# Softmax stage of a hybrid decoder layer: columns of maxima and inverse sums turned by one transpose each and spread by DMA

## The reference, cut to what is computed here

```python
z = jnp.einsum('bhqd,bhkd->bhqk', qi, k).astype(jnp.float32) * scale
causal = key_pos[None, :] <= q_pos[:, None]
p = jax.nn.softmax(jnp.where(causal, z, neg), axis=-1)
return jnp.einsum('bhqk,bhkd->bhqd', p.astype(v.dtype), v)
```

## Time and profile before

| | us |
|---|---|
| median of three runs | 2100.22 |
| the profiled execution's own time | 2099.88 |
| its span in the trace | 2098.2 |
| softmax stage, first score matmul of a turn | 1397.0 |
| softmax stage, last store issued | 1896.4 |

### The profile page before, as it was taken

One profiled execution on the slowest core, in us unless ns is written; L12 is line 12 of the kernel. 1 busy time (PEld: TensorE's weight loads), 2 busy tenths in 40 slices (PEclk: granted clock), 3 DMA queues, 4 the chain that ended last, 5 costly groups with the idle time before them and its releaser, 6 DMA issues. The chain is left out here.

```text
span 2098.2 us, 32790 instructions
## 1 busy us (share of the span) xinstructions
PE 1890.4 (90%) x9697; PEld 1543.5 (74%) x9697; DVE 1235.8 (59%) x1862; ACT 953.7 (45%) x1894; POOL 1019.9 (49%) x1035
## 2 busy tenths in 40 slices
PE   6479999997999999499998989769999999996998
PEld 1358888885999998367776767548888787875776
DVE  1742111113555556398989989568888889882101
ACT  1521111113333333167777767547777777771000
POOL 0400000000343434169998989937887878781212
PEclk9589999998999999599999999969999999997999
DMA  8326554354455554660624525162254541604564
GB/s 305 106 81 180 161 167 133 105 186 172 165 182 180 192 180 154 161 137 25 154 69 105 116 60 127 51 135 51 51 121 91 115 97 44 178 21 144 177 197 143
DMA packets 225691, 273.69 MB, mean 130 GB/s; under 512 B 13840, under 2 KB 161584, under 8 KB 220192
## 3 DMA queue, kind: packets, MB, share of 16 engines
q1 hardware_dynamic: 219936, 259.24, 43.7%
q10 hardware_dynamic: 5632, 13.11, 1.9%
HBM read 159.06 MB, written 109.05 MB: 128 GB/s over the span
## 5 line engine op out<-in xcount | busy, mean ns | idle before, releaser
L1983 POOL TENSOR_TENSOR mla_wl<-mla_w,mla_wh 128x512 fp32r<-128x512 f32 (+1 forms) x320 | 380.4, 1205 | 109.2 <-ACT mla_wh L2019 103.8
L1492 POOL TENSOR_TENSOR sb_wl<-sb_wf,sb_wh 128x512 fp32r<-128x512 f32 (+2 forms) x240 | 286.2, 1193 | 19.2
L1595 DVE TENSOR_TENSOR_SCAN sb_w<-sb_kp,sb_w,sb_beside 128x512 f32<-128x512 f32 x192 | 245.4, 1278 | 30.1 <-ACT sb_kp L1518 12.3
L2018 ACT ACTIVATE mla_w<-mla_zt 128x512 f32<-128x512 f32 (+1 forms) x320 | 171.0, 534 | 112.5 <-PE mla_zt L2169 55.3
L570 PE MATMUL pt_po<-h_hi,pt_wh 128*128 128x512 f32 x512 | 200.1, 391 | 9.0 <-DVE pt_wl L501 9.0
L571 PE MATMUL pt_po<-h_lo,pt_wh 128*128 128x512 f32 x512 | 199.9, 390 | 0.0
L572 PE MATMUL pt_po<-h_hi,pt_wl 128*128 128x512 f32 x512 | 199.9, 390 | 0.0
L2060 DVE TENSOR_REDUCE mla_nmx<-mla_zn 128x1 f32<-128x512 f32 (+2 forms) x320 | 191.6, 601 | 5.6 <-PE mla_zn L2139 3.1
L1518 ACT ACTIVATE sb_kp<-sb_z 128x512 f32<-128x512 f32 (+3 forms) x320 | 169.4, 531 | 39.0 <-DVE sb_w L1595 13.4
L1707 PE MATMUL sb_pt<-sb_ident,sb_w 128*128 128x128 f32 x1088 | 174.1, 275 | 9.6 <-DVE sb_wl L1604 9.5
L83 POOL MEMSET tk_ident<- 128x128 f32 x1 | 0.2, 205 | 372.6 <-POOLq L62 372.6
(11 more groups left out here) (229 smaller groups left out, 4338.2 us busy)
## 6 DMA issues: line engine op xcount, KB each, us to landing
mod_wada<-in_w_ada SPq DMA_DIRECT2D x6, 2048.0 KB, 8.5
qk_mla<-tk_th SPq DMA_DIRECT2D x64, 192.0 KB, 2.1
qk_mla<-tk_tl SPq DMA_DIRECT2D x64, 192.0 KB, 2.3
mod_x<-in_x ACTq DMA_DIRECT2D x16, 512.0 KB, 4.3
pt_w<-in_w_feat SPq DMA_DIRECT2D x16, 512.0 KB, 5.9
hT<-h_hi SPq DMA_DIRECT2D x16, 512.0 KB, 3.6
hT<-h_lo SPq DMA_DIRECT2D x16, 512.0 KB, 5.2
qk_sb<-pt_oh SPq DMA_DIRECT2D x32, 256.0 KB, 2.6
```

The source lines that it names most:

```text
L1492: nc.gpsimd.tensor_tensor(wl[i][:, lo:GW], wf[i][:, lo:GW], wh[i][:, lo:GW].bitcast(F32), ALU.subtract).then_inc(s_plo, 1)
L1595: nc.vector.tensor_tensor_scan(kept, keeps, beside[:, 0:b - a], 1.0 if u["n"] == 0 else w[u["g"]][:, u["r"], b:b + 1], ALU.mult, ALU.bypas ...
L1983: nc.gpsimd.tensor_tensor(wl[i][:, cols], w[i][:, cols], wh[i][:, cols].bitcast(F32), ALU.subtract).then_inc(s_lo, 1)
L2018: nc.scalar.activation(w[i][:, cols], zt[x % 2][:, cols], ACT.Exp).then_inc(s_w, 1)
```

## The change

The row of maxima and the spread of inverse sums no longer go through four transposes and a ScalarE copy each:

- One transpose turns nm (128 x 4) into 4 x 128 in PSUM (`turn_max`). VectorE copies it to SBUF (`lines_max`). SyncE writes it to a scratch tensor `maxima` in DRAM, four pieces of 512 bytes, waits for that to land, and reads it back as one row of 512 into row 96 of q (`to_row`, now on SyncE). All of this sits 21 slots ahead of the group's end.
- The same for inv: `turn_inv` and `lines_inv` at LAG + 1, then `spread` on SyncE, a write to `inverses`, a wait for its landing, and a read that is broadcast to 64 partitions of `scale`.
- ScalarE's steps `row` and `totals` are gone. ps has 128-column fields for sums and both turned tiles.
- AHEAD goes from 20 to 22; quotient from LAG + 3 to LAG + 6, mh and ml from LAG + 5 and LAG + 6 to LAG + 8 and LAG + 9. nm stays at -AHEAD.
- SyncE now walks the slots too, in the order row, loads, spread, store: q and k loads for the next head at slot 0, values at slot 4, gate at slot 13 of the first head of a pair (with the output weights in the last pair), stores at LAG + 9.

```diff
-    delays = dict(nm=-AHEAD, pm=2 - AHEAD, row=2 - AHEAD, sum=LAG, inv=LAG, spread=LAG + 1, half=LAG, sums=LAG + 1, add=LAG,
-                  gate=LAG, quotient=LAG + 3, mh=LAG + 5, ml=LAG + 6)
+    delays = dict(nm=-AHEAD, turn_max=1 - AHEAD, lines_max=1 - AHEAD, row=1 - AHEAD, sum=LAG, inv=LAG, turn_inv=LAG + 1,
+                  lines_inv=LAG + 1, spread=LAG + 1, half=LAG, add=LAG, gate=LAG, quotient=LAG + 6, mh=LAG + 8, ml=LAG + 9,
+                  store=LAG + 9)
+            def to_row(it, hp, n):
+                g, head = plan.groups[n]["g"], it * 2 + hp
+                sp.wait_ge(s_lmax, groups(n, it, hp) + 1)
+                sp.dma_start(maxima[bass.ds(head, 1), n, :].rearrange("o (r p) -> (o r) p", p=P),
+                             lines_m[n % 2][:].bitcast(F32)).then_inc(s_max_out, 16)
+                sp.wait_ge(s_max_out, 16 * groups(n, it, hp) + 16)
+                sp.dma_start(qh[hp][QK:KP, g * GW:(g + 1) * GW].bitcast(F32), maxima[bass.ds(head, 1), n, :]
+                             ).then_inc(s_row[n % 2], 16)
+            def spread(it, hp, n):
+                sp.wait_ge(s_linv, groups(n, it, hp) + 1)
+                sp.dma_start(inverses[bass.ds(head, 1), n, :].rearrange("o (r p) -> (o r) p", p=P), lines_i[:]
+                             ).then_inc(s_inv_out, 16)
+                sp.wait_ge(s_inv_out, 16 * groups(n, it, hp) + 16)
+                reached(sp, s_scale, 16 * groups(n, it, hp))
+                reached(sp, s_quot, pair_groups(n, it - 1) + 1)
+                sp.dma_start(scale[hb:hb + HD, g * GW:(g + 1) * GW],
+                             inverses[bass.ds(head, 1), n, :].broadcast_to([HD, GW])).then_inc(s_scale, 16)
+            def loads(it, hp, x):
+                last = isinstance(it, int) and it == PAIRS - 1
+                if x == 0 and not (last and hp == 1):
+                    reached(sp, s_zt, turns(0, it, hp))
+                    load_qk(it + hp, 1 - hp)
+                if x == LAG + 1 and not (last and hp == 1):
+                    reached(sp, s_pv, turns(0, it, hp))
+                    load_v(it + hp, 1 - hp)
+                if x == TAIL + 1 and hp == 0:
+                    reached(sp, s_gated, pair_groups(0, it))
+                    sp.dma_start(gate[:], gates[bass.ds(it, 1), :, :].rearrange("o p n -> p (o n)")).then_inc(s_gate, 16)
+            run(sp, dict(row=to_row, turn=loads, spread=spread, store=store))
-            def totals(it, hp, n):
-                nc.scalar.activation(scale[hb:hb + HD, g * GW:(g + 1) * GW], ps[hb:hb + HD, :],
-                                     ACT.Copy).then_inc(s_scale, 1)
+            def lines_max(it, hp, n):
+                dve.wait_ge(s_tmax, groups(n, it, hp) + 1)
+                reached(dve, s_max_out, 16 * (groups(n, it, hp) - 1))
+                nc.vector.tensor_copy(lines_m[n % 2][:], turned_max).then_inc(s_lmax, 1)
+            def lines_inv(it, hp, n):
+                dve.wait_ge(s_tinv, groups(n, it, hp) + 1)
+                reached(dve, s_inv_out, 16 * groups(n, it, hp))
+                nc.vector.tensor_copy(lines_i[:], turned_inv).then_inc(s_linv, 1)
             def quotient(it, hp, n):
-                dve.wait_ge(s_scale, groups(n, it, hp) + 1)
+                dve.wait_ge(s_scale, 16 * groups(n, it, hp) + 16)
                 if tn["first"]:
-                    pe.wait_ge(s_row, groups(tn["n"], it, hp) + 1)
+                    pe.wait_ge(s_row[tn["n"] % 2], 16 * rows(tn["n"], it, hp) + 16)
+            def turn_max(it, hp, n):
+                pe.wait_ge(s_nm, groups(n, it, hp) + 1)
+                nc.tensor.transpose(turned_max, nm[n % 2][:], ident[:]).then_inc(s_tmax, 1)
+            def turn_inv(it, hp, n):
+                pe.wait_ge(s_inv, groups(n, it, hp) + 1)
+                nc.tensor.transpose(turned_inv, inv[n % 2][:], ident[:]).then_inc(s_tinv, 1)
```

More of the change, by code:

```diff
@@ L1788, in at, with attend_mla @@
         return found
-def attend_mla(nc, t, qkS, vS, gates, mix, shared, wout):
+def attend_mla(nc, t, qkS, vS, gates, mix, shared, wout, maxima, inverses):
     plan = Turns()
@@ L1826, in attend_mla @@
         nm = [m.sb(f"nm{i}", [P, QG]) for i in range(2)]
+        lines_m = [m.sb(f"lines_m{i}", [QG, P], F32R) for i in range(2)]
+        lines_i = m.sb("lines_i", [QG, P])
         half = m.sb("half", [P, GW])
         om = m.sb("om", [P, S])
-        inv = m.sb("inv", [P, QG])
+        inv = [m.sb(f"inv{i}", [P, QG]) for i in range(2)]
         scale = m.sb("scale", [P, S])
@@ L1849, in attend_mla @@
         s_nm = m.sem("nm")
-        s_pm = m.sem("pm")
-        s_row = m.sem("row")
+        s_tmax = m.sem("tmax")
+        s_lmax = m.sem("lmax")
+        s_tinv = m.sem("tinv")
+        s_linv = m.sem("linv")
+        s_max_out = m.sem("max_out")
+        s_row = [m.sem(f"row{i}") for i in range(2)]
         s_zt = m.sem("zt")
@@ L1879, in pair_groups, with rows @@
             return it * G + n
+        def rows(n, it, hp):
+            return it * G + (hp * (G // 2) + n // 2)
         def run(eng, steps):
@@ L1916, in load_v, with store @@
                              ).then_inc(s_v[hp], 16)
-            def store(it, n):
+            def store(it, hp, n):
+                if hp == 0:
+                    return
                 sp.wait_ge(s_ml, pair_groups(n, it) + 1)
@@ L1927, in _ @@
             sp.dma_start(kl[0][0:QK, :].rearrange("p (n c) -> p n c", n=NB).bitcast(F32),
                          qkS[1, 1, :, :, 0:P].rearrange("n p c -> p n c")).then_inc(s_qkl[0], 16)
[L1930 to L1953, removed]
@@ L2051, in high @@
                 nc.scalar.activation(mh[n % 2][:], om[:, cols], ACT.Copy).then_inc(s_mh, 1)
-            run(act, dict(row=row, turn=weights, half=v_low, sums=totals, mh=high))
+            run(act, dict(turn=weights, half=v_low, mh=high))
         @block.vector
@@ L2123, in _ @@
                                           zeros[QK:KP, :].unsqueeze(1).broadcast_to([1, NB, P])).then_inc(s_rows, 1)
-            run(dve, dict(piece=maximum, nm=row_maximum, turn=add_up, inv=inverse, add=halves, quotient=quotient, ml=low))
+            run(dve, dict(piece=maximum, nm=row_maximum, lines_max=lines_max, lines_inv=lines_inv, turn=add_up, inv=inverse, add=halves,
+                          quotient=quotient, ml=low))
         @block.tensor
@@ L2143, in piece @@
                 mm.then_inc(s_zn, 1)
[L2145 to L2153, removed]
             def scores(it, hp, x):
@@ L2186, in product @@
                 nc.tensor.matmul(out, vj, wl[x % RING][:, lo:GW], start=False, stop=tn["last"]).then_inc(s_pv, 1)
+            def turn_max(it, hp, n):
+                pe.wait_ge(s_nm, groups(n, it, hp) + 1)
+                reached(pe, s_lmax, groups(n, it, hp))
+                if n < 2:
+                    reached(pe, s_linv, groups(n, it, hp) - (2, 1)[n])
+                nc.tensor.transpose(turned_max, nm[n % 2][:], ident[:]).then_inc(s_tmax, 1)
+            def turn_inv(it, hp, n):
+                pe.wait_ge(s_inv, groups(n, it, hp) + 1)
+                reached(pe, s_linv, groups(n, it, hp))
+                nc.tensor.transpose(turned_inv, inv[n % 2][:], ident[:]).then_inc(s_tinv, 1)
             def over_keys(it, hp, n):
                 pe.wait_ge(s_acc, turns(plan.groups[n]["end"], it, hp) + 1)
-                reached(pe, s_scale, groups(n, it, hp))
-                rows = groups(n, it, hp) + (2 if n == G - 1 else 3)
-                reached(pe, s_row, min(rows, 2 * PAIRS * G) if isinstance(rows, int) else rows)
+                if n in (1, 3):
+                    pe.wait_ge(s_linv, groups(n, it, hp))
+                else:
+                    rows_out = groups(n, it, hp) + (4 if n == 0 else 3)
+                    pe.wait_ge(s_lmax, min(rows_out, 2 * PAIRS * G) if isinstance(rows_out, int) else rows_out)
                 for r in range(QG):
-                    mm = nc.tensor.matmul(ps[:, r:r + 1], acc[n % 2][:, r * P:(r + 1) * P], ones[:, 0:1],
+                    mm = nc.tensor.matmul(sums[:, r:r + 1], acc[n % 2][:, r * P:(r + 1) * P], ones[:, 0:1],
                                           start=True, stop=True)
                 mm.then_inc(s_sum, 1)
[L2201 to L2208, removed]
+            run(pe, dict(piece=piece, turn_max=turn_max, turn_inv=turn_inv, turn=scores, product=product, sum=over_keys))
 def output(nc, t, keep, mix_sb, mix_mla, out, wout):
@@ L2339, in build @@
     mix_mla = scratch("mix_mla", (2, H // 2, P, S))
+    maxima = scratch("maxima", (H, GROUPS, GW))
+    inverses = scratch("inverses", (H, GROUPS, GW))
     with ExitStack() as ctx:
@@ L2364, in build @@
                                for k in range(KD)], sems[3])
-            attend_mla(nc, t, qk_mla, v_mla, gates[4:8], mix_mla, shared, wout)
+            attend_mla(nc, t, qk_mla, v_mla, gates[4:8], mix_mla, shared, wout, maxima, inverses)
         output(nc, t, keep, mix_sb, mix_mla, out, wout)
```

40 lines of the change are left out of this document (21 added, 19 removed).

## The result

The changed kernel takes 2159.86 us (median of four runs, 2157.40 to 2162.37). The ratio to the kernel before is 1.0279, 95% interval 1.0261 to 1.0297: slower by 59 us. The forecast was 2157.

What follows compares the result with a forecast made beforehand. TensorE was taken to set the pace, about 61 us a head. From 2099.9 us: -20 transposes, +2 VectorE, +58.5 stalls, +12 clock, +2.5 start, +2.2 end gave 2157.1; range 2105 to 2190.

Steps and rivals of the forecast that it cites:

- Transposes, 20 us off: On TensorE in the softmax stage, six fewer transposes in each of 32 groups, 0.103 us each, save 20 us.
- Where the stalls are: At head starts: TensorE waits for its row in heads 1, 3, 5; VectorE's quotient waits for scale in 2, 4, 6.
- Their size, 58.5 us: Stalls at head starts: 10.3 us in each of heads 1, 3, 5 and 9.2 in each of 2, 4, 6.
- Part 1: The prediction's step on TensorE's transposes, priced by duration: 20 us off a full engine.
- Clock, 12 us: TensorE's granted clock drops with each of six stalls, costing a further 2 us each; bounds 0 and 24.
- VectorE, 2 us: Added copies on VectorE make TensorE's waits for it, 7.9 us, grow by 2; bounds 0 and 8.
- start, 2.5: At the stage's start, the first turn waits for the first row's round trip: 2.5 us more.
- end, 2.2: At the stage's end, the last quotient waits for the last inverse's round trip: 2.2 us more; bounds 1.5 and 4.
- A: Rival: loads don't hold small transfers up at head starts, or finish in time; 2086.6 us, faster; chance 0.15.
- B: Rival: waits at head starts are half as long, 30 us, and the clock stays up; 2117 us; chance 0.17.
- D: Rival: n = 0's row also late in seven heads, or clock low long after stalls; 2190 to 2230 us; chance 0.12.
- LOADS: Theory stated for the experiments: small transfers at head starts stand behind the next head's loads.

Runs made afterwards that it cites:

- e4_small_late: The changed kernel with loads of q, k and values for heads 2 to 7 cut to one partition and both new transposes behind turn and product: 2104.0 us.
- f3_wout: f1_split with the PSUM users of tile ps in slots of their own and the output weights loaded in the last head: 2097.3 us, ratio 0.9990.
- e2_late: The changed kernel with turn_max and turn_inv on TensorE behind the turn and product of their slot instead of ahead: 2157.0 us.
- e1_small: The changed kernel with loads of q, k and values for heads 2 to 7 cut to one partition each: 2135.4 us.
- f4_act: f3_wout with the copies of the turned tiles on ScalarE instead of VectorE: 2101.3 us.
- e6_actq_late: The changed kernel with small transfers on ScalarE's DMA queue, write and read in different slots, and both new transposes behind turn and product: 2149.2 us.
- f1_split: The changed kernel with both new transposes behind turn and product and each head's loads in 16 parts of 256 KB, gate and output weights also split: 2113.3 us.
- b1_small: The kernel before the change with loads of q, k and values for heads 2 to 7 cut to one partition each: 2101.8 us.
- f5_pool: f3_wout with the quotient on GpSimd instead of VectorE: 2107.1 us.
- b2_pool: The kernel before the change with the quotient on GpSimd instead of VectorE: 2112.1 us.

## Why the prediction came out right, and where it was wrong

The total was right within 3 us, the direction and most places too. Three of its terms were not, and that they cancelled is luck: stalls counted some 40 us too high, against 21 us of waits that had no term and a clock loss 24 us too low.

- *Transposes, 20 us off.* Right as a price: 2.4 and 2.6 us in an undisturbed head (e4_small_late, f3_wout). In the kernel as changed it is real but hidden behind the stalls, and even in the best version only 7.2 us of the stretch come out.
- *Where the stalls are.* Right for five of six: VectorE's quotient in heads 2, 4 and 6, the row in 3 and 5, and the order on SyncE to the step. Head 1's row held TensorE up by 0.3 us only; in e2_late it did by 5.9. Head 2's read of scale was forecast to land at t0 + 24.6; the quotient started at 1553.00, t0 + 24.8.
- *Their size, 58.5 us.* Too large by more than two: the five stalls are 23.8 us. Beyond the 8 us of the earlier trace rows, the first and third kind of PE's wait give some 19 us. The terms that were too large: a small round trip, 2.1 us a transfer assumed, takes 1.3 to 1.4, and the values load alone 6.0 instead of 8.0. So head 3's row was in at about t0 + 28.5 and not 32.9, and slot 16 came later than forecast.
- *No price for the place of the transposes.* This is the step that failed: a term put at nothing. Part 1 gave them a duration and not a position. before had an interval of two slots between nm and its transposes, and had those of inv behind the product; after has one slot, and both ahead of the turn. TensorE stood idle for 21 us by it. With the two transposes behind the turn, e2_late, the waits for inv and nm fell from 18.2 us to 1.1 (those for the copies rose from 2.9 to 5.6), and where the loads were cut as well, that edit brought 31 us (e1_small to e4_small_late).
- *Clock, 12 us.* Too small by a factor of three: 36 by busy time. The forecast took six stalls, each with 2 us behind it. The clock also fell after stretches with only short waits, at the end of head 0 and in the middle of head 1 among them (last section).
- *VectorE, 2 us; start, 2.5; end, 2.2.* The copies cost nothing (f4_act). The first turn started at 1399.9, 2.9 after before's; from the last transpose to the output stage 18.5 for 16.2 us, 2.3 more. Head 7, forecast 2.5 us shorter, was 1.2 longer, and head 0 2.8 longer.
- *The rivals.* A (the loads hold nothing up) fell, as the writes of 7.6 and 9.2 us made TensorE wait; its own sign, landings under 11 us, was met and didn't decide it. B (waits half as long, 30 us) was nearest on the stalls' size and wrong on the clock, which it had staying up. D's extra waits for rows did not come; the extra waits that came were VectorE's. LOADS, as stated for the experiments, was too narrow in one point: it is the loads in flight, not the shared queue alone, that hold a small transfer up (e6_actq_late).

## What to carry to other kernels

Whoever takes work off the engine that sets the pace and pays with a round trip through DRAM has to look at what else is in flight at each trip, on all queues, and at what stands behind the waiting instruction; here large loads in parts of 256 KB were worth 44 us (f1_split against e2_late). An operation on a full engine has a position as well as a duration: ask of each one that is moved or new what it waits for there. And two causes can hide each other: one edit gave 3 us, the other 24, both 56.

## What the runs showed of the hardware

- A write of four pieces of 512 bytes takes 1.3 to 1.4 us from issue to the next step on an idle queue (after). Beside the full loads in pieces of 512 bytes it takes 7.6 and 9.2 in their queue (after) and 6.9 in another (e6_actq_late), beside their parts of 256 KB 2.1 (f1_split, head 3).
- TensorE's granted clock fell also where no wait was longer than 1.0 us. In heads 0 and 1 of after it is low in these three stretches (columns as in the earlier trace rows):

```profile
1400.00:1410.00 10.00, 10.00 (x28) 7.91 (x27) 5.94 (x10) 5.15 (x10) 5.10 (x4) 0.53 1.20 233
...
1461.00:1468.00 7.00, 7.00 (x24) 5.95 (x23) 3.51 (x8) 2.62 (x6) 1.82 (x4) 0.55 0.47 119
...
1495.00:1499.00 4.00, 4.00 (x14) 3.15 (x13) 2.72 (x5) 1.38 (x3) 3.05 (x3) 0.62 0.00 1
```

The first is carried over from ahead of the stage, and before starts its turns so as well (0.50 from 1397 to 1403). The other two are falls in the middle of full work: in the 6 us ahead of 1461 PE was busy 5.4, with no wait over 0.7 us, and in the 5 us ahead of 1495 4.3, with none over 0.4. The early waits are of this size, and e1_small, which had them and no long stall, ran the stage at 0.95; that they cause the falls was not tested apart from the rest. b1_small, with the waits of before, had 0.98 in the turns' stretch and was 4 us longer there, at the same median; so a few us of any one profile's clock are chance, but 36 are not.
- A VectorE operation with two inputs in SBUF, 0.68 us at its fastest, took up to 1.8 us in before and 6.06 us in f5_pool and 6.03 in b2_pool, both while GpSimd ran back to back.
